# Weight slots and feature arrays at other byte phases in SBUF

## The chip, the cores and the metric

The kernel runs on one core of one Trainium2 chip, as one launch. The metric is device microseconds for the whole launch, the median of repeated executions. TensorE (PE) multiplies, VectorE (DVE), ScalarE (ACT) and GpSimd (POOL) do the elementwise work, SyncE (SP) and ScalarE issue DMAs. SBUF has 128 partitions; an address in this text is the byte offset within a partition, and "phase" is that address modulo 128 (or modulo 512, where said).

## What is computed

Two networks of layers on 512 tokens of 1024 features, all in float32. The first has four layers, each a mixer, a feed-forward block and a gated embedding; the second is one layer with a retention, a linear recurrence and a feed-forward block. Cut to what fills the time:

```python
for i in range(DEPTH):                       # DEPTH = 4
    y = mixer_i(h)                           # diff_attention, hgrn2, swa_sink_attention, diff_attention
    h = layer_norm(ALPHA * h + y, ln_g[i, 0], ln_b[i, 0])
    u = jnp.square(jax.nn.relu(h @ w_up[i])) @ w_down[i]      # 1024 -> 4096 -> 1024
    h = layer_norm(ALPHA * h + u, ln_g[i, 1], ln_b[i, 1])
    h = h + jax.nn.sigmoid(h @ w_ple_gate[i]) * (p[i] @ w_ple[i])
...
z = rms_norm_2(x, norm1_w) @ w_in            # second network: eight projections,
                                             # retention, RG-LRU, merge, feed-forward of 3072
```

Every large product is a projection: features (512 tokens) times a weight matrix that is read once from HBM.

## The kernel before

**Slabs.** All weights come as a stream of 287 slabs (`stream`, `N_SLABS`). A slab is 128 partitions x 8 x 256 floats (1 MB): 8 chunks k of 128 input features, for 256 output features. `Plan` lists them in the order of use; a unit is the work on one slab that ends in two PSUM banks.

**Slots.** A slab lives in one of four slots (`SLOT`, `make_slots`). A slot has two arrays of 8 KB a partition: `raw` (the slab as it lands), over which `wlo` is written in place, and `whi`. `place_slot` lays them out, one after the other; slots 0, 1 and 2 stand first in SBUF, slot 3 behind the constants. For slabs 211 to 249 slot 3 is used for other data and three slots turn.

**Split precision.** A float32 product is made of three float32r products. For the weights, SP's DMA fills `raw` (L433, after `unit_done` shows that the slot's previous slab is no longer needed); POOL rounds it into `whi` (L467; for 13 slabs ACT does it, L1340); DVE subtracts, `wlo = raw - whi` (L1767), and signals `split_done`, on which PE waits at the start of a unit (`begin_unit`). The features have two parts as well: `xh` and `xl`, `gh` and `gl`, 8 chunks of 512 floats each.

**Matmul shapes.** `feature_chunk` (L497 to L499 through `passes`): weights stationary (128x128), features moving, 512 columns; 48 matmuls a slab. `half_chunk` (L618 to L620): the same with 256 tokens at a time, used around the norms; 48 a slab for each half. `token_chunk` (L530 to L532): features stationary, 256 columns of weights moving; 96 a slab. In program order one matmul follows the other, high x high, high x low, low x high, and the weight load of each runs beside the matmul before it. Of 512 columns there are 8,976 matmuls from slots 0 to 2 and 2,160 from slot 3 (L497 to L499); of 256 columns 3,264 from slots 0 to 2 (2,304 in half chunks, 960 in token chunks) and 1,536 from slot 3 (960 and 576).

**Where a unit stands.** In a feed-forward block the slabs turn through the slots in order. In layer 0's block slab 18 (slot 2), 19 (slot 3), 20 (slot 0), 21 (slot 1), 22 (slot 2) and 23 (slot 3) are used in whole units one after the other, from 291.56 us of the profile on.

**Addresses.** `place` puts arrays one after the other from byte 16512, rounded up to 32 bytes. So raw0, whi0, raw1, whi1, raw2, whi2, h, xh, xl, gh and gl all lie at 128 modulo 512 (phase 0 modulo 128). The array `vec` has a size that is no multiple of 128; what stands behind it (ident, ones, small, raw3 at 151232, whi3 at 159424 and the arena of the mixers) lies at 192 modulo 512, phase 64 modulo 128. Each chunk of weights is 1024 bytes behind the one before, each chunk of features 2048, and the second half of a slab's outputs 512, so chunks have the phase of their array. No phase enters the order of work: it is written out by hand, with semaphores between the engines, and stays as it is.

Of the kernel before, what the change touches and what calls it, by code (L numbers as in the profile page):

```python
# [18 lines left out]
F32 = mybir.dt.float32  # L19
F32R = mybir.dt.float32r  # L20
# [4 lines left out]
P = 128  # L25
# [14 lines left out]
LAM_INIT = [0.8 - 0.6 * math.exp(-0.3 * i) for i in (0, 3)]  # L40
RD = 639
RING = 4

# [69 lines left out]
def make_slots():  # L115

    slots, users = [], {i: -1 for i in range(RING)}
    three = range(PLAN.at["ret"][0] + 2, PLAN.at["wout"][0] + 3)
# [8 lines left out]
SLOT = [s for s, _ in SLOTS]  # L127
# [17 lines left out]
def cols(hf):  # L145
    return slice(0, S) if hf is None else slice(hf * HALF, (hf + 1) * HALF)
# [64 lines left out]

def build(nc, stream, xin, pin, pos, vecs, relb, onehot, eye, picks, decay, out):
    with ExitStack() as ctx:
        top = [16512]

        def place(name, shape, dt=F32, at=None):

            size = (int(np.prod(shape[1:])) * 4 + 31) // 32 * 32
            if at is None:
                at, top[0] = top[0], top[0] + size  # L220
            assert at + size <= nc.sbuf_usable_end, (name, at, size)
            return nc.alloc_sbuf_tensor_at(name, shape, dt, offset=at)

        raw, wlo, whi = [], [], []

        def place_slot(i):
            at = top[0]
            raw.append(place(f"raw{i}", [P, 8, 256]))
            wlo.append(place(f"wlo{i}", [P, 8, 256], F32R, at=at))
            whi.append(place(f"whi{i}", [P, 8, 256], F32R))  # L230

        for i in range(3):
            place_slot(i)
        h = place("h", [P, KT, S])
        hg_m = place("hg_m", [P, 2, S], at=top[0] + 6 * S * 4)
        xh = place("xh", [P, KT, S], F32R)
# [5 lines left out]
        ident = place("ident", [P, P])  # L242
        ones = place("ones", [P, P])
        small = place("small", [P, 256])
        fourth = top[0]
        place_slot(3)
        arena = top[0]

# [10 lines left out]
        a = Arena()  # L259
# [7 lines left out]
        a = Arena(ln_end)  # L267
# [3 lines left out]
        a = Arena(ln_end)  # L271
# [5 lines left out]
        pair_end = a.at - arena  # L277
        sg = Arena(sg_at)("sg", [P, 2, 2, S])

        a = Arena()  # L280
# [12 lines left out]
        a = Arena()  # L293
# [13 lines left out]
        a = Arena()  # L307
# [9 lines left out]
        a = Arena(fourth - arena)  # L317
# [10 lines left out]
        rt_z = a("rt_z", [P, 2, S])  # L328
        rt_t = Arena(rt_z_at)("rt_t", [P, 2, S])
        rt_o = a("rt_o", [P, 4, 256])  # L330
        assert a.at - arena >= pair_end
        cosf = a("cosf", [P, S])
        sinf = a("sinf", [P, S])

# [2 lines left out]
        a = Arena(fourth - arena)  # L337
# [7 lines left out]
        a = Arena(ln_end)  # L345
# [4 lines left out]
        a = Arena(40 * 1024)  # L350
# [3 lines left out]
        a = Arena(sq_at)  # L354
# [14 lines left out]
        def sem(name):  # L369
            return ctx.enter_context(nc.semaphore(name))  # L370

        raw_in = [sem(f"raw_in{i}") for i in range(RING)]
        hi_done, hi_act = sem("hi_done"), sem("hi_act")
# [15 lines left out]
        def M(name):  # L389
            if name not in m:  # L390
                m[name] = sem(name)
            return m[name]
# [23 lines left out]
        @block.sync  # L416
        def _(sp):

            for t in range(4):
                sp.dma_start(raw[0][:, 2 * t:2 * t + 2].rearrange("p k n -> p (k n)"), stream[0, :, 512 * t:512 * t + 512]).then_inc(first_in[t], 16)  # L420
            for n in range(1, N_SLABS):
                if n < 3:
                    sp.wait_ge(x_in[n + 1], 16)
                elif n == 3:
                    sp.wait_ge(raw_in[2], 16)
                else:
                    sp.wait_ge(unit_done, PLAN.last_unit[BEFORE[n]] + 1)
                if n == RETURNED:
                    sp.wait_ge(gl_ready, 4 * (G_GEN["mixed"] + 1))
                if n == 2:  # L430
                    for dst, src in (vec[:, :], vecs), (ident[:, :], eye), (tab[:, :], onehot), (rb[0:32, :], relb):
                        sp.dma_start(dst, src).then_inc(loaded, 16)
                sp.dma_start(raw[SLOT[n]][:, :, :].rearrange("p k n -> p (k n)"), stream[n]).then_inc(raw_in[SLOT[n]], 16)  # L433

            for hf in range(2):
                for t in range(KT // 2):
                    p2 = slice(2 * t, 2 * t + 2)
                    sp.wait_ge(M("final_out"), KT // 2 * hf + t + 1)
                    sp.dma_start(out[:, p2, cols(hf)], fin[:, p2, cols(hf)]).then_inc(M("stored"), 16)
            sp.wait_ge(M("stored"), KT * 16)  # L440
# [2251 lines left out]
```

## Time and profile before

| | |
|---|---|
| median of 3 runs | 3551.46 us (3550.85 to 3552.41) |
| span of the profiled execution | 3552.2 us |
| PE busy | 3512.9 us (99%) |
| PE weight loads busy | 2952.0 us (83%) |
| DVE busy | 1766.9 us (50%) |
| ACT busy | 960.4 us (27%) |
| POOL busy | 632.3 us (18%) |
| granted TensorE clock | 0.998 of full |
| PE's share of the chain that ended last | 88% |

Busy time of PE is the union of its matmuls from issue to end. A matmul overlaps the next one, so its own duration (391 ns in the mean for 512 columns) is more than what it adds to the time. What it adds is the distance between starts, or a stretch of the profile divided by its matmuls.

### The profile page before, as it was taken

Reading aid. Unit: us, or ns where it says so; the run is one execution under the profiler, and the core shown is the slowest. Engines: PE = TensorE matmul, PEld = TensorE weight load, DVE = VectorE, ACT = ScalarE, POOL = GpSimd, SP = SyncE. Lnnn points to the kernel's source line nnn. Section 1 sums busy time; section 2 is a strip of 40 time slices with the busy share of each in tenths; the row PEclk is TensorE's granted clock in tenths of the full one; section 3 lists DMA queues with packets and bytes.
Section 4 is the critical chain, followed back from the end, with each engine's and each line's share of the span. In section 5 each row is a group of like instructions: output and inputs, shape, how many; then the busy total and the mean of one; then the engine's idle time right before and its main releaser. Section 6 shows DMA issues by size and latency. Waiting matters only on the chain.

```text
span 3552.2 us, 44299 instructions
## 1 busy us (share of the span) xinstructions
PE 3512.9 (99%) x18416; PEld 2952.0 (83%) x18416; DVE 1766.9 (50%) x2276; ACT 960.4 (27%) x1679; POOL 632.3 (18%) x372
## 2 busy tenths in 40 slices
PE   9999999999999999999999999999999999999999
PEld 7788888889888888688888878888888888898887
DVE  5454334556653346763336445553474346563434
ACT  3562001334220013630013256210141215120102
POOL 2112111200131112031112111311121111211110
PEclk9999999999999999999999999999999999999999
DMA  5322222222222223122222221222222222322222
GB/s 205 107 78 90 95 95 92 104 85 85 70 100 95 95 83 111 59 89 95 95 95 95 101 84 72 98 95 95 83 77 102 72 95 95 107 95 95 95 95 71
DMA packets 65463, 332.88 MB, mean 94 GB/s; under 512 B 9795, under 2 KB 20291, under 8 KB 28532
## 3 DMA queue, kind: packets, MB, share of 16 engines
q1 hardware_dynamic: 44316, 303.50, 23.8%
q10 hardware_dynamic: 20952, 26.56, 2.3%
q8 instruction: 149, 2.44, 0.3%
q14 instruction: 46, 0.38, 0.0%
HBM read 326.22 MB, written 10.90 MB: 95 GB/s over the span
## 4 chain that ended last, share of the span: by engine, by line
PE 88%; DVE 6%; ACT 4%; issue 1%; POOL 1%; DMA 0%; DVEq 0%; ACTq 0%; POOLq 0%
PE proj L497 23%; PE proj L499 23%; PE proj L498 23%; PE proj L618 2%; PE proj L619 2%; PE proj L620 2%; PE proj L530 2%; PE proj L532 2%; PE proj L531 2%; DVE wlo L1767 1%; PE mix L708 1%; DVE s L1877 1%; ACT xh L1182 1%; ACT h L1185 1%; PE mix L734 1%
## 5 line engine op out<-in xcount | busy, mean ns | idle before, releaser
L467 POOL TENSOR_SCALAR whi<-raw 128x2048 fp32r<-128x2048 f32 x272 | 528.8, 1944 | 2689.9 <-DVE wlo L1767 1722.1
L497 PE MATMUL proj<-gh,whi 128*128 128x512 f32 x1952 | 777.6, 398 | 2.2 <-DVE wlo L1767 2.2
L499 PE MATMUL proj<-gh,wlo 128*128 128x512 f32 x1952 | 763.5, 391 | 0.0
L498 PE MATMUL proj<-gl,whi 128*128 128x512 f32 x1952 | 762.8, 391 | 0.0
L1767 DVE TENSOR_TENSOR wlo<-raw,whi 128x2048 fp32r<-128x2048 f32 x285 | 651.3, 2285 | 137.9 <-POOL whi L467 95.2
L497 PE MATMUL proj<-xh,whi 128*128 128x512 f32 x1760 | 695.4, 395 | 8.9 <-DVE wlo L1767 3.1
L498 PE MATMUL proj<-xl,whi 128*128 128x512 f32 x1760 | 688.5, 391 | 0.0
L499 PE MATMUL proj<-xh,wlo 128*128 128x512 f32 x1760 | 688.4, 391 | 0.0
L497 PEld LDWEIGHTS proj<-gh,whi 128*128 128x128 f32 x1952 | 367.0, 188 | 95.1 <-issue 15.6
L499 PEld LDWEIGHTS proj<-gh,wlo 128*128 128x128 f32 x1952 | 366.9, 188 | 80.0
L498 PEld LDWEIGHTS proj<-gl,whi 128*128 128x128 f32 x1952 | 367.1, 188 | 77.7 <-issue 1.9
L497 PEld LDWEIGHTS proj<-xh,whi 128*128 128x128 f32 x1760 | 330.8, 188 | 92.5 <-issue 11.6
L499 PEld LDWEIGHTS proj<-xh,wlo 128*128 128x128 f32 x1760 | 330.9, 188 | 72.1
L498 PEld LDWEIGHTS proj<-xl,whi 128*128 128x128 f32 x1760 | 331.1, 188 | 70.9 <-issue 1.4
L1486 ACT ACTIVATE rl<-proj 128x1024 f32<-128x1024 f32 x64 | 65.8, 1028 | 957.1 <-PE proj L499 938.5
L1860 DVE TENSOR_TENSOR h<-h,proj 128x1024 f32<-128x1024 f32 (+1 forms) x76 | 80.0, 1053 | 351.8 <-PE proj L499 329.3
L2301 DVE SCALAR_TENSOR_TENSOR hid<-proj,rl 128x1024 f32<-128x1024 f32 x64 | 78.4, 1225 | 322.7 <-ACT rl L1486 322.2
L618 PE MATMUL proj<-xh,whi 128*128 128x256 f32 x608 | 174.3, 287 | 4.2 <-POOL xl L462 2.8
L619 PE MATMUL proj<-xl,whi 128*128 128x256 f32 x608 | 171.3, 282 | 0.0
L620 PE MATMUL proj<-xh,wlo 128*128 128x256 f32 x608 | 171.2, 282 | 0.0
L530 PE MATMUL proj<-whi,gh 128*128 128x256 f32 x512 | 149.0, 291 | 0.0
L532 PE MATMUL proj<-whi,gl 128*128 128x256 f32 x512 | 144.1, 282 | 0.0
(321 smaller groups left out, 4324.0 us busy)
## 6 DMA issues: line engine op xcount, KB each, us to landing
raw<-in_stream SPq DMA_DIRECT2D x286, 1024.0 KB, 4.8
da_b<-bias_da ACTq DMA_DIRECT2D x16, 512.0 KB, 3.4
bias_da<-bias_rows ACTq DMA_DIRECT2D x8, 512.0 KB, 8.8
h<-in_x ACTq DMA_DIRECT2D x4, 512.0 KB, 8.9
bias_sw<-bias_table ACTq DMA_DIRECT2D x1, 2048.0 KB, 9.9
pf<-in_p ACTq DMA_DIRECT2D x4, 512.0 KB, 6.8
sw_b<-bias_sw ACTq DMA_DIRECT2D x4, 512.0 KB, 3.6
out_features<-fin SPq DMA_DIRECT2D x8, 256.0 KB, 2.5
```

What stands on the lines that cost most here:

```text
L467: nc.gpsimd.tensor_scalar(whi[SLOT[n]][:, :, :], raw[SLOT[n]][:, :, :], 1.0, 0.0, ALU.mult, ALU.add).then_inc(hi_done, 1)
L497: nc.tensor.matmul(out, wh, ah, start=first, stop=False, skip_group_check=check)
L498: nc.tensor.matmul(out, wh, al, start=False, stop=False, skip_group_check=check)
L499: return nc.tensor.matmul(out, wl, ah, start=False, stop=last, skip_group_check=check)
L530: nc.tensor.matmul(o, ah, wh, start=k == 0 and st % per == 0, stop=False, skip_group_check=True)
L532: last = nc.tensor.matmul(o, al, wh, start=False, stop=k == kn - 1, skip_group_check=True)
L618: nc.tensor.matmul(o, wh, ah, start=k == 0 and (j if own_banks else hf) == 0, stop=False, skip_group_check=True)
L619: nc.tensor.matmul(o, wh, al, start=False, stop=False, skip_group_check=True)
L620: last = nc.tensor.matmul(o, wl, ah, start=False, stop=k == 7, skip_group_check=True)
L1767: V.tensor_tensor(wlo[SLOT[n]][:, :, :], raw[SLOT[n]][:, :, :], whi[SLOT[n]][:, :, :].bitcast(F32), ALU.subtract).then_inc(*own.sig(split_ ...
L1860: ins = V.tensor_tensor(o, o, y, ALU.add)
L2301: V.scalar_tensor_tensor(hid[:, :, :], banks(u), 0.0, rl[:, :, :], ALU.max, ALU.mult).then_inc(*own.sig(rel["dve"]))
```

## The change

The arrays of the slots get other addresses, in SBUF alone: what is loaded, computed and stored, and the order on every engine, are the same.

```diff
+STARTS = ((32, 64), (0, 0), (0, 0), (0, 256))
+ROWS = (256, 260, 258, 256)
...
-        top = [16512]
+        top = [16896]
...
         def place_slot(i):
-            at = top[0]
-            raw.append(place(f"raw{i}", [P, 8, 256]))
-            wlo.append(place(f"wlo{i}", [P, 8, 256], F32R, at=at))
-            whi.append(place(f"whi{i}", [P, 8, 256], F32R))
+            (lo, hi), row = STARTS[i], ROWS[i]
+            size = 8 * 4 * row
+            wide = [f(name, [P, 8, row], dt, at=top[0] + at) for f, name, dt, at in
+                    ((place, f"raw{i}", F32, lo), (place, f"wlo{i}", F32R, lo), (place, f"whi{i}", F32R, lo + size + hi))]
+            for slots, tile in zip((raw, wlo, whi), wide):
+                slots.append(tile[:, :, 0:256])
+            top[0] += (2 * size + lo + hi + 127) // 128 * 128
 
         for i in range(3):
             place_slot(i)
+        top[0] = (top[0] + 511) // 512 * 512
         h = place("h", [P, KT, S])
...
         small = place("small", [P, 256])
+        top[0] = (top[0] + 511) // 512 * 512
         fourth = top[0]
         place_slot(3)
...
-        assert a.at - arena >= pair_end
+        a.at = max(a.at, arena + pair_end)
...
-                sp.dma_start(raw[SLOT[n]][:, :, :].rearrange("p k n -> p (k n)"), stream[n]).then_inc(raw_in[SLOT[n]], 16)
+                sp.dma_start(raw[SLOT[n]][:, :, :], stream[n].rearrange("p (k n) -> p k n", k=8)).then_inc(raw_in[SLOT[n]], 16)
```

What comes out, modulo 128, for chunk k of a slab:

| | raw, wlo before | whi before | raw, wlo after | whi after |
|---|---|---|---|---|
| slot 0 | 0 | 0 | 32 | 96 |
| slot 1 | 0 | 0 | 16k | 16k |
| slot 2 | 0 | 0 | 8k | 64 + 8k |
| slot 3 | 64 | 64 | 0 | 0 (256 modulo 512) |

Modulo 512, h, xh, xl, gh and gl go from 128 to 0; ident, ones and small from 192 to 64; the arena of the mixers from 192 to 256. In slots 1 and 2 a partition of a slab is no longer one run of 8192 bytes but eight of 1024 with 16 or 8 bytes between them, so its DMA has 1,024 pieces in place of 128, and POOL's, ACT's and DVE's operands are 8 x 256 in place of 2048 elements. Slots 0 and 3 stay contiguous.

## Rows read from the trace of the kernel before

**Rows 1.** The page: busy time by engine; the chain that ended last.

```profile
PE 3512.9 (99%) x18416; PEld 2952.0 (83%) x18416; DVE 1766.9 (50%) x2276; ACT 960.4 (27%) x1679; POOL 632.3 (18%) x372
...
PE 88%; DVE 6%; ACT 4%; issue 1%; POOL 1%; DMA 0%; DVEq 0%; ACTq 0%; POOLq 0%
```

**Rows 2.** Groups of PE's matmuls: count, busy us, mean ns, idle before and who ended it.

```profile
L497 PE MATMUL proj<-gh,whi 128*128 128x512 f32 x1952 | 777.6, 398 | 2.2 <-DVE wlo L1767 2.2
...
L497 PE MATMUL proj<-xh,whi 128*128 128x512 f32 x1760 | 695.4, 395 | 8.9 <-DVE wlo L1767 3.1 <-DVE xl L2167 2.5 <-POOL xl L462 1.6
```

**Rows 3.** Stretches of one slab, 48 matmuls of 512 columns: slots 3, 0, 1, 3.

```profile
core 0: us, PE busy (x) PEld busy (x) DVE busy (x) ACT busy (x) POOL busy (x), PEclk, DMA share, GB/s
...
302.47:313.67 11.20, 11.20 (x49) 9.02 (x48) 5.79 (x4) 2.09 (x2) 2.83 (x1) 1.00 0.26 96
313.67:324.58 10.91, 10.91 (x50) 9.01 (x48) 4.65 (x3) 2.09 (x2) 1.92 (x1) 1.00 0.27 96
324.58:335.46 10.88, 10.88 (x50) 9.01 (x48) 3.42 (x2) 0.00 (x0) 1.92 (x1) 1.00 0.28 96
...
346.34:357.54 11.20, 11.20 (x50) 9.02 (x48) 3.42 (x2) 0.00 (x0) 1.91 (x1) 1.00 0.24 94
```

**Rows 4.** Timeline in slot 3, then slot 1 (start us, us); then groups of the two slabs.

```profile
307.84 0.39 PE L499 MATMUL proj<-xh,wlo 128*128 128x512 f32 x1
308.07 0.40 PE L497 MATMUL proj<-xh,whi 128*128 128x512 f32 x1
308.31 0.39 PE L498 MATMUL proj<-xl,whi 128*128 128x512 f32 x1
...
329.79 0.39 PE L499 MATMUL proj<-gh,wlo 128*128 128x512 f32 x1
330.02 0.39 PE L497 MATMUL proj<-gh,whi 128*128 128x512 f32 x1
...
L497 PE MATMUL proj<-xh,whi 128*128 128x512 f32 x16 | 6.3, 396 | 0.0
...
L497 PE MATMUL proj<-gh,whi 128*128 128x512 f32 x16 | 6.2, 389 | 0.0
```

**Rows 5.** Stretches with 256 columns: slots 2, 3, 3 (48 matmuls); 0, 3 (96).

```profile
598.66:604.41 5.75, 5.75 (x50) 5.75 (x48) 5.41 (x4) 1.15 (x2) 0.00 (x0) 1.00 0.49 182
618.02:623.48 5.46, 5.46 (x51) 5.46 (x49) 4.84 (x9) 3.91 (x8) 1.48 (x2) 1.00 0.55 195
604.41:610.06 5.65, 5.65 (x50) 5.65 (x49) 5.41 (x5) 0.64 (x1) 1.92 (x1) 1.00 0.01 3
2668.91:2680.43 11.52, 11.52 (x99) 11.52 (x97) 8.79 (x6) 1.03 (x1) 3.80 (x2) 1.00 0.29 95
704.67:715.98 11.31, 11.31 (x97) 11.30 (x96) 0.00 (x0) 1.09 (x2) 0.00 (x0) 1.00 0.26 94
```

**Rows 6.** Timeline of PE where the weights of the next slab are late.

```profile
2990.72 0.39 PE L499 MATMUL proj<-xh,wlo 128*128 128x512 f32 x1
2992.66 0.50 PE L497 MATMUL proj<-gh,whi 128*128 128x512 f32 x1 [1.55 <-DVE wlo L1767]
```

**Rows 7.** DMA issues: count, KB each, median us to landing; then POOL's group.

```profile
raw<-in_stream SPq DMA_DIRECT2D x286, 1024.0 KB, 4.8
da_b<-bias_da ACTq DMA_DIRECT2D x16, 512.0 KB, 3.4
...
sw_b<-bias_sw ACTq DMA_DIRECT2D x4, 512.0 KB, 3.6
...
L467 POOL TENSOR_SCALAR whi<-raw 128x2048 fp32r<-128x2048 f32 x272 | 528.8, 1944 | 2689.9 <-DVE wlo L1767 1722.1 <-DMA raw<-in_stream 922.8 <-DVE s L1877 44.9
```

**Rows 8.** DVE: the split of a slab (min/median/max ns), and two shapes of 512.

```profile
L1767 DVE TENSOR_TENSOR wlo<-raw,whi x285: 2260/2285/2318, 23.9 to 3508.4; 128x2048 fp32r<-128x2048 f32 x143
...
L1921 DVE TENSOR_TENSOR h<-h,mix 128x512 f32<-128x512 f32 x48 | 33.0, 688 | 3.7 <-DVE h L1923 0.5
...
L2125 DVE TENSOR_TENSOR hg_q<-hg_q,hg_t 128x512 f32<-128x512 f32 x24 | 16.5, 688 | 13.0 <-PE mix L815 13.0
```

## The prediction, made before the result was known

> **What bounds the kernel now.** I read the page first: PE is busy for 3512.9 of 3552.2 us and holds 88% of the chain of work that ended last, while DVE (50%), ACT (27%), POOL (18%) and the DMA engines have room [rows 1]. The reader should see that a faster DVE, POOL or DMA gives nothing here, and that a change which moves nothing but addresses can only tell in the spacing of PE's matmuls. So I took the spacing apart next. Two shapes fill PE: 11,136 matmuls of 512 columns (six groups of 1952 or 1760, of which two stand in [rows 2]) and 4,800 of 256 columns. The means there are from issue to end of one matmul, which overlaps the next; the spacing has to be read from the starts, or from how long a slab of 48 matmuls lasts.
>
> The table of stretches gives that for single slabs in one steady feed-forward run, at full granted clock [rows 3]. A slab of 48 matmuls of 512 columns takes 10.88 us from slot 1 (226.7 ns each), 11.20 us from slot 3 (233.3 ns each), and 10.91 us from slot 0 right after slot 3. Nothing waits in any of them, and PE does the same work. DVE, ACT and POOL are busy to different degrees in these stretches, but slabs from slot 3 later in the same run cost 11.20 again with ACT idle (346.34 to 357.54), so their company is not the cause. The timeline shows it matmul by matmul: starts 0.23 us apart for slot 1, 0.23 or 0.24 for slot 3, and the means from issue to end, 389 ns against 396, say the same [rows 4].
>
> What sets slot 3 apart is its address. By the placement code raw0 to whi2 and xh, xl, gh, gl all lie at 128 modulo 512; raw3 and whi3 lie at 192 modulo 512, so 64 bytes off the features that stream through. In the 256-column shapes the sign turns [rows 5]: a slab of 48 takes 5.75 us (119.8 ns each) from slot 2, but 5.65 or 5.46 from slot 3; a slab of 96 token matmuls takes 11.52 from slot 0 and 11.31 from slot 3. So the phase of weights against features is worth 3% of a matmul, either way by shape. That is the only lever the change has.
>
> **How fast a 512-column matmul can be.** The matmul of L499 at 2990.72 us (slot 2) has no weight load beside it, because the next slab is late and the next matmul starts 1.94 us on [rows 6]: it still takes 0.39 us, like those of slot 1 in rows 4. So 226.7 ns looks like the pace of the moving stream alone, not a loss to weight loads that a better phase could give back. I take it as the floor for this shape. For 256 columns the floor shown is 5.46 us for a slab (113.7 ns).
>
> The Trainium skill (SBUF — State Buffer, "Who interferes with whom"; TensorE: Matmul & The Clock Gate, "Step-by-step: what each phase is for") says that the moving operand and LDWEIGHTS have independent read ports and that PE never waits on anyone. By that rule no placement could change PE's spacing, and the whole change would be worth its DMAs only; the 11.20 beside 10.88 in rows 3 speaks against it.
>
> **The change part by part.**
> - *Slot 3 to 0 and 256, features to multiples of 512.* The phase against the features becomes 0 modulo 128, like slots 0 to 2 before. 2,160 matmuls of 512 columns use slot 3: 45 slabs x (11.20 - 10.88) = 14.4 us gained. That 256 modulo 512 acts like 0 is an assumption; the trace holds no such pair, so the bounds are 14.4 and 0. The 256-column slabs of slot 3 lose what they had: 20 slabs of 48 x 0.10 to 0.29, I take 0.2, so 3.9 us; 6 token slabs x 0.21 = 1.3 us. Together 5.2 lost.
> - *Slots 0 to 2 off phase, 512 columns.* This is the large term: 8,976 matmuls, 187 slabs, now at the floor of 10.88. Slot 0: whi at 96, wlo at 32. Slot 1: rows of 1040 bytes, so chunk k starts at 16k modulo 128. Slot 2: rows of 1032 bytes, 8k for wlo and 64 + 8k for whi. The trace shows only 0 and 64. Bounds per slab: 0 (all of these act like 0) and 0.32 (all act like 64). Two readings put it between. If what counts is which half of 128 bytes a weight row starts in, slot 0 has two of three matmuls in the far half, slot 1 half of them, slot 2 two of three: about 0.6 x 0.32 = 0.19. And the slab after slot 3 pays 0.03 us to settle after one change of phase [rows 3]; slots 1 and 2 now change phase at each of 8 chunks, 8 x 0.03 = 0.24. I take 0.20: 187 x 0.20 = 37.4 us lost. Ends: 0 and 59.8.
> - *Slots 0 to 2, 256 columns.* 48 slabs of 48 and 10 of 96, now at the slow end. With the same share of 0.6 towards slot 3's times: 48 x 0.6 x 0.2 + 10 x 0.6 x 0.21 = 7.1 us gained. Ends: 0, and 48 x 0.29 + 10 x 0.21 = 16.0.
> - *DMAs of slots 1 and 2.* The row in SBUF is no longer contiguous, so a slab that came in 128 pieces of 8 KB comes in 1,024 of 1 KB. The nearest rows: 512 KB in 1 KB pieces (sw_b) lands in 3.6 us, in 2 KB pieces (da_b) in 3.4; a slab in 8 KB pieces in 4.8 [rows 7]. That puts a slab at some 5.2 to 7.2 us. The cover is PE itself: a slab is asked for when its slot is let go, two or three slabs of 10.88 us ahead, and PE waited for wlo 2.2 + 3.1 us in all [rows 2]. The slabs that are already late (one stands in rows 6) can lose half a microsecond each: 1 us lost, ends 0 and 6. If the cover were gone, each of 150 slabs would pay 0.4 to 2.4.
> - *DVE, POOL and ACT on rows of 260 and 258.* The split of a slab takes 2260 to 2318 ns on DVE over all slots, so slot 3's phase does nothing there, and an operation over two runs of 256 elements (L1921, 688 ns) costs what a run of 512 does (L2125, 688 ns) [rows 8]. Taken at 0; POOL is idle most of the time and waits 1722 us for DVE [rows 7], so even 10% on its 1944 ns would be hidden. The arena moves from 64 to 0 modulo 128 while ident, ones and small stay at 64: some hundreds of small matmuls, each a few ns either way, taken at 0 with 1 us on both sides.
>
> Sum: -14.4 + 5.2 + 37.4 - 7.1 + 1.0 = +22.1 us. The profiled execution (3552.2 us) is 0.7 above the median of 3551.46, so the shift goes on the median: 3551.5 + 22.1 = **3573.6 us**.
>
> **The rivals.**
> 1. *Every phase settles at the floor, and the time falls.* If what costs is exactly an offset of 64, and the others let the stream settle as at 0, slots 0 to 2 lose nothing at 512 columns and slot 3 gains. Then -14.4 + 5.2 + 1.0, and the 256-column slabs give 0 to 16: 3527 to 3543. For it: slot 3 shows that phases exist which are faster at 256 columns, and only one phase is shown slow at 512. Against: a slab needs 0.03 us to settle after one change, and slots 1 and 2 change at each chunk. It decides when the off-phase slabs cost less than about 0.08 us over 10.88, since 187 x 0.08 = 15 is what the other terms give back. The Trainium skill (SBUF — State Buffer, "Specifications (TRN2)") gives SBUF lines of 16 bytes, with a penalty for each crossing to a new one; by that, slots 0 and 1, whose rows start at multiples of 16, would cost nothing, and no row here shows a line of that size.
> 2. *Worse than slot 3.* A single matmul in slot 3 takes 0.23 or 0.24 by turns; its mean of 233.3 ns is then made of turns of about 231 and 236. If an odd phase holds the slow turn, a slab takes 11.33: 187 x 0.45 = 84, and the time is about 3605 to 3635.
> 3. *No change.* Only if the slot 3 effect comes from something other than the phase, or the terms cancel (share of 0.2 in place of 0.6): 3551.5 + 1 = 3552, within 7 us. The Trainium skill's rule of independent ports, named above, gives the same time.
> 4. *The DMAs bind.* 1 KB pieces slow a slab beyond the cover: PE's waits for wlo would grow from 5.3 us to tens, in the stretch with three slots (2700 to 3110 us) first. 3575 to 3600; small, since even with three slots the cover is 2 x 10.88 - 4.8 - 1.9 - 2.3 = 12.8 us (slab, load, POOL and DVE from rows 3, 7 and 8).
>
> **How the numbers follow.** The forecast case (a loss of 0.1 to 0.32 us a slab in slots 0 to 2: 3558 to 3600) gets 0.47. Rival 1 gets 0.25, rival 2 0.10, rival 3 0.14, rival 4 0.04. A range that holds 8 in 10 starts inside rival 1, at 3530, and ends at the bound of the forecast case with a slot 3 that gains little, 3605. The likeliest case alone: 3558 to 3600. A measurement here tells about 0.2% (7 us) from no change: faster than 3544.4 in 0.25, within in 0.15 (rival 3 and an edge of the forecast case), slower than 3558.6 in 0.60.
>
> **What would show it.** In the changed profile, 48-matmul slabs in the same feed-forward run: slot 3 at 10.88 (right) or still 11.20 (256 does not act like 0); slots 0, 1, 2 at 11.0 to 11.2, and within slots 1 and 2 a spacing that differs from chunk to chunk. 256-column slabs from slots 0 to 2 between 5.46 and 5.75. DVE's split still 2285 ns, slab DMAs 5 to 7 us, PE's waits for wlo below 10 us. The prediction is wrong if slots 0 to 2 stay at 10.88, or if they go below it: then 226.7 ns was no floor, and the gain would be of a size that nothing above allows for.

## The result, and the profile of the changed kernel

The changed kernel takes 3589.02 us (3587.55 to 3589.61, 4 runs) beside 3551.81 us (3550.85 to 3552.41, 4 runs) of the kernel before on the same chip: ratio 1.0103, 95% interval 1.0089 to 1.0116, so 37.2 us slower. The profiled execution has a span of 3587.6 us, where before had 3552.2. Direction and mechanism were as predicted, and the time is inside the range. The shift was put at 22.1 us, so its largest term had been put too small.

The page of the changed kernel, to be read beside [rows 1], [rows 2] and [rows 7]: busy time by engine; the queue of the slabs (packets, MB, share of 16 engines); the chain that ended last; a group of matmuls; the slabs' DMA. L497 to L499 of before are L504 to L506 here.

```profile
PE 3549.2 (99%) x18416; PEld 2952.2 (82%) x18416; DVE 1764.6 (49%) x2276; ACT 960.3 (27%) x1679; POOL 631.9 (18%) x372
...
q1 hardware_dynamic: 178716, 303.50, 25.4%
...
PE 87%; DVE 6%; ACT 4%; issue 1%; POOL 1%; DMA 0%; DVEq 0%; ACTq 0%; POOLq 0%
...
L504 PE MATMUL proj<-gh,whi 128*128 128x512 f32 x1952 | 785.1, 402 | 1.8 <-DVE wlo L1774 1.8
...
raw<-in_stream SPq DMA_DIRECT2D x286, 1024.0 KB, 5.5
```

PE is 36.3 us longer busy (3512.9 before) with the same 18,416 matmuls; DVE, ACT and POOL do what they did. A matmul of the group takes 402 ns from issue to end where it took 398. The table below shows that the shift of 35.4 us in the span is PE's spacing.

Stretches of one slab in the same feed-forward block of layer 0 (columns as in [rows 3]): slots 3, 0, 1, 2 at 512 columns; then 48 matmuls of 256 columns from slots 2 and 3, and 96 token matmuls from slot 3.

```profile
303.15:314.04 10.89, 10.89 (x50) 9.01 (x48) 5.79 (x4) 2.09 (x2) 2.82 (x1) 1.00 0.32 99
314.04:325.31 11.27, 11.27 (x49) 9.02 (x48) 4.65 (x3) 2.09 (x2) 1.92 (x1) 1.00 0.26 93
325.31:336.48 11.17, 11.17 (x49) 9.03 (x48) 3.42 (x2) 0.00 (x0) 1.90 (x1) 1.00 0.26 94
336.48:347.64 11.16, 11.16 (x50) 9.02 (x48) 3.42 (x2) 0.00 (x0) 1.90 (x1) 1.00 0.32 95
...
603.40:609.08 5.68, 5.68 (x49) 5.67 (x48) 5.34 (x4) 1.15 (x2) 0.00 (x0) 1.00 0.60 185
609.08:614.84 5.76, 5.76 (x51) 5.76 (x50) 5.52 (x5) 0.63 (x1) 1.91 (x1) 1.00 0.01 3
710.19:721.70 11.51, 11.51 (x98) 11.51 (x97) 0.00 (x0) 1.09 (x2) 0.00 (x0) 1.00 0.30 93
```

The roles have changed: slot 3, 11.20 before [rows 3], is now at 10.89, and slots 0, 1 and 2, 10.88 to 10.91 before, are at 11.27, 11.17 and 11.16. At 256 columns slot 3 is now the slow one (5.76, and 11.51 for a token slab, 11.31 before [rows 5]) and slot 2 gains a little (5.68, 5.75 before).

What PE waited for (us in total, times, longest), and DVE's split of a slab (min/median/max ns):

```profile
PE proj L504 <- DVE wlo L1774: 3.9, 7, 1.4
```

```profile
L1774 DVE TENSOR_TENSOR wlo<-raw,whi x285: 2260/2284/2319, 25.1 to 3543.7; 128x2048 fp32r<-128x2048 f32 x143
```

PE's waits for `wlo` are not longer than before (3.9 us in all, where [rows 2] had 2.2 and 3.1), and the split takes what it took [rows 8].

Where the time went, by laying the matmuls of both profiles side by side in program order and adding up the differences between starts (only where neither has a gap behind it):

| | matmuls | mean spacing before, after (ns) | us |
|---|---|---|---|
| slot 0, 512 columns | 2,922 | 227.6, 234.4 | +19.8 |
| slot 1, 512 columns | 2,955 | 227.1, 232.7 | +16.4 |
| slot 2, 512 columns | 2,923 | 227.3, 232.3 | +14.8 |
| slot 3, 512 columns | 2,163 | 233.2, 227.1 | -13.2 |
| slot 3, 256 columns | 1,481 | | +4.7 |
| slots 0 to 2, 256 columns | 3,120 | | -4.8 |
| all the rest, gaps included | | | -2.0 |
| sum | | | +35.7 |

The sum runs from the start of the first matmul to the start of the last. Within slot 1 the mean spacing of a chunk lies between 230.1 and 235.3 ns, within slot 2 between 229.6 and 234.7. Chunk 0 of slot 1, whose `whi` lies at the features' phase and whose `wlo` lies 128 bytes off, has 232.8 ns.

### The profile page after: what moved, and what is told of

The parts are those of the page before. It is cut to its first block, busy times and chain, and to the rows that moved or that the text cites. A ratio compares the mean times of both kernels' runs of the same rounds, so it can differ in the third digit from the quotient of the medians.

```text
span 3587.6 us, 44299 instructions
## 1 busy us (share of the span) xinstructions
PE 3549.2 (99%) x18416; PEld 2952.2 (82%) x18416; DVE 1764.6 (49%) x2276; ACT 960.3 (27%) x1679; POOL 631.9 (18%) x372
## 4 chain that ended last, share of the span: by engine, by line
PE 87%; DVE 6%; ACT 4%; issue 1%; POOL 1%; DMA 0%; DVEq 0%; ACTq 0%; POOLq 0%
PE proj L504 23%; PE proj L506 23%; PE proj L505 23%; PE proj L625 2%; PE proj L626 2%; PE proj L627 2%; PE proj L537 2%; PE proj L538 2%; PE proj L539 2%; DVE wlo L1774 1%; PE mix L715 1%; DVE s L1884 1%; ACT xh L1189 1%; ACT h L1192 1%; PE mix L741 1%
## 5 line engine op out<-in xcount | busy, mean ns | idle before, releaser
L504 PE MATMUL proj<-gh,whi 128*128 128x512 f32 x1952 | 785.1, 402 | 1.8 <-DVE wlo L1774 1.8
L506 PE MATMUL proj<-gh,wlo 128*128 128x512 f32 x1952 | 770.3, 395 | 0.0
L505 PE MATMUL proj<-gl,whi 128*128 128x512 f32 x1952 | 769.7, 394 | 0.0
L504 PE MATMUL proj<-xh,whi 128*128 128x512 f32 x1760 | 700.3, 398 | 7.2 <-DVE xl L2174 2.5
L506 PE MATMUL proj<-xh,wlo 128*128 128x512 f32 x1760 | 693.3, 394 | 0.0
L505 PE MATMUL proj<-xl,whi 128*128 128x512 f32 x1760 | 692.8, 394 | 0.0
L504 PEld LDWEIGHTS proj<-gh,whi 128*128 128x128 f32 x1952 | 367.3, 188 | 100.8 <-issue 15.6
L506 PEld LDWEIGHTS proj<-gh,wlo 128*128 128x128 f32 x1952 | 367.7, 188 | 87.2
L505 PEld LDWEIGHTS proj<-gl,whi 128*128 128x128 f32 x1952 | 367.1, 188 | 84.3 <-issue 1.9
L504 PEld LDWEIGHTS proj<-xh,whi 128*128 128x128 f32 x1760 | 330.7, 188 | 95.4 <-issue 11.1
L506 PEld LDWEIGHTS proj<-xh,wlo 128*128 128x128 f32 x1760 | 331.0, 188 | 77.7
L505 PEld LDWEIGHTS proj<-xl,whi 128*128 128x128 f32 x1760 | 330.5, 188 | 75.9 <-issue 1.4
L538 PE MATMUL proj<-wlo,gh 128*128 128x256 f32 x512 | 144.3, 282 | 0.0
```

Of the source, the lines that this page charges most:

```text
L504: nc.tensor.matmul(out, wh, ah, start=first, stop=False, skip_group_check=check)
L505: nc.tensor.matmul(out, wh, al, start=False, stop=False, skip_group_check=check)
L506: return nc.tensor.matmul(out, wl, ah, start=False, stop=last, skip_group_check=check)
L538: nc.tensor.matmul(o, ah, wl, start=False, stop=False, skip_group_check=True)
```

## The experiments

Theory at the start: the spacing of PE's matmuls follows from the distance in bytes between the array of the weights and that of the features, and the slabs' DMAs and the other engines add nothing. Rival theories: the absolute address counts; the change of phase from chunk to chunk costs; the shorter DMA pieces cost. Each kernel is the kernel before with the edit shown. "At d" means that a weight array lies d bytes off the features.

**Slot 3 alone, at the features' phase.**

```diff
+        def align(phase):
+            top[0] += (128 + phase - top[0]) % 512
...
+        align(0)
         fourth = top[0]
         place_slot(3)
```

> The kernel before with slot 3 moved to 128 modulo 512, the phase of the features and of the other slots; everything else stays (the arena moves with it). If the relation of weights to features is what counts, slot 3's slabs of 48 matmuls of 512 columns go from 11.20 to 10.88 us (45 slabs, 14 us) and its 256-column slabs from 5.46 or 5.65 to 5.75 and from 11.31 to 11.52 (5 us lost): 3542 to 3544 us. If slot 3 was slow for another reason (its place behind the constants, its neighbours in the arena), it stays at 11.20 and the time at 3551.

Measured: 3540.06 beside 3552.74 us, ratio 0.9965 (0.9952 to 0.9977): 12.7 us faster. Slots 2 and 3 in the feed-forward block:

```profile
335.04:345.92 10.88, 10.88 (x50) 9.01 (x48) 3.42 (x2) 0.00 (x0) 1.91 (x1) 1.00 0.28 98
345.92:356.80 10.88, 10.88 (x50) 9.01 (x48) 3.42 (x2) 0.00 (x0) 1.92 (x1) 1.00 0.25 96
```

Slot 3's 512-column matmuls give 13.5 us, its 256-column ones take 4.7, and some 4 us of the two spans' difference come from elsewhere (1.4 us from the spacing in slots 0 to 2, whose slab behind slot 3 took 10.91, the rest from gaps). The first term of the prediction stands, and it is the part of the change that was worth having.

**The 1 KB pieces alone.** The stream is stored with rows of 260 elements for slots 1 and 2, so that their slabs go in 1,024 pieces to the old, contiguous places.

```diff
+                if SLOT[n] in (1, 2):
+                    of = of.rearrange("p (k n) -> p k n", k=8)[:, :, 0:256]
```

> The kernel before with only the DMAs of slots 1 and 2 in 1 KB pieces: in HBM the chunks of a row stand 1040 bytes apart, in SBUF nothing moves. If the DMAs carry a part of the loss of 37 us, the time is above 3555. If they are covered by PE, as the theory of phases says, landing goes from 4.8 to some 6 us and the time stays within 2 us of 3552.

Measured: 3552.82 beside 3552.74 us, ratio 1.0002 (0.9993 to 1.0011). Its queue and the DMA of a slab:

```profile
q1 hardware_dynamic: 178716, 303.50, 26.0%
...
raw<-in_stream SPq DMA_DIRECT2D x286, 1024.0 KB, 5.4
```

As many packets as in the changed kernel, a landing 0.6 us later than before [rows 7], and no time beyond the interval of -2.5 to +3.9 us: the DMAs are out as the cause of 37 us.

**One phase for all chunks of a slot, by turns.** Both kernels keep rows of 256 elements and shift whole slots: slots 0 to 3 at 16, 32, 48, 0 in one, at 80, 96, 112, 8 in the other.

```diff
+PHASE = (16, 32, 48, 0)
...
+            align(PHASE[i] // 32 * 32)
```

> Slots 0, 1 and 2 at 16, 32 and 48 bytes past the phase of the features, rows of 256, so that phase is the same in every chunk and for whi and wlo; slot 3 at the features' phase. A theory that the changes of phase from matmul to matmul cost (0.03 us each) gives 10.88 to 10.91 us a slab in all four slots, and some 3540 us. A theory that the phase itself costs gives 11.0 to 11.3 us for slots 0 to 2 and 10.88 for slot 3, near 3575.

> The same with slots 0 to 3 at 80, 96, 112 and 8 bytes past the features. If changes of phase cost, all four at 10.88 to 10.91 us and some 3540 us. If the phase itself costs, 11.0 to 11.3 us a slab, slot 3 with its 8 bytes too, near 3585. If only the 64-byte half counts, 8 is like 0 (10.88) and the others like 64 (11.20).

Measured in one execution each: 3575.49 and 3596.18 us, beside 3552.74. Stretches of slots 0, 1, 2 of the first, then 0 to 3 of the second, in the feed-forward block:

```profile
314.05:324.94 10.89, 10.89 (x49) 9.01 (x48) 4.65 (x3) 2.09 (x2) 1.91 (x1) 1.00 0.27 96
324.94:336.13 11.19, 11.19 (x49) 9.01 (x48) 3.42 (x2) 0.00 (x0) 1.92 (x1) 1.00 0.26 94
336.13:347.33 11.20, 11.20 (x49) 9.12 (x48) 3.42 (x2) 0.00 (x0) 1.91 (x1) 1.00 0.26 95
```

```profile
314.50:325.64 11.14, 11.14 (x49) 9.01 (x48) 4.65 (x3) 2.09 (x2) 1.93 (x1) 1.00 0.23 94
325.64:336.89 11.25, 11.25 (x50) 9.04 (x48) 3.42 (x2) 0.00 (x0) 1.92 (x1) 1.00 0.26 93
336.89:348.09 11.20, 11.20 (x50) 8.98 (x49) 3.42 (x2) 0.00 (x0) 1.90 (x1) 1.00 0.26 95
348.09:359.16 11.07, 11.07 (x50) 9.02 (x49) 3.42 (x2) 0.00 (x0) 1.92 (x1) 1.00 0.26 95
```

A slot at 32 or 48 costs 11.19 and 11.20 with the same phase in all its chunks, as much as slots 1 and 2 of the changed kernel (11.17, 11.16), whose phase changes at each chunk. So no change of phase from chunk to chunk is needed for this price. Nor does it turn on the half of 128 bytes in which a row begins: 32 costs what 64 did.

**Everything at one other phase.** All slots, the features and the arena are moved by 64 bytes together.

```diff
+PHASE = (64, 64, 64, 64)
...
+        align(64)
```

> All four slots and the features 64 bytes on, at 192 modulo 512, rows of 256. If the relation of weights to features counts, all slots take 227 ns a matmul at 512 columns and the time is 3540 us. If the address itself counts (a weight row that starts in the second half of 128 bytes), all slots take 233 ns: 11,136 x 6.3 = 70 us more, near 3605.

Measured: 3541.62 us in one execution, within 2 us of the kernel with slot 3 aligned, at another absolute address. Slot 0 and slot 3:

```profile
311.62:322.50 10.88, 10.88 (x49) 9.01 (x48) 4.65 (x3) 2.09 (x2) 1.91 (x1) 1.00 0.26 96
...
344.26:355.14 10.88, 10.88 (x49) 9.01 (x48) 3.42 (x2) 0.00 (x0) 1.91 (x1) 1.00 0.27 96
```

So the absolute address is out: what counts is how far the weights lie from the features.

**The parts of the change, each alone.** Both kernels are the changed one with one table set back: slot 0's part without the rows, and the rows without slot 0's part.

```diff
-ROWS = (256, 260, 258, 256)
+ROWS = (256, 256, 256, 256)
```

> The changed kernel with rows of 256 in every slot: slot 0 keeps 32 and 96, slots 1 to 3 are at the features' phase. From the spacing in the changed kernel, slot 0's 2928 matmuls of 512 columns cost 7.3 ns each more (21 us) and its 256-column ones give 2 us back, so if the parts add up this is 3540 + 19 = 3559 to 3561 us. If the losses of the changed kernel come from jumps between slots of different phase instead, slot 0 alone costs less than 10 us.

```diff
-STARTS = ((32, 64), (0, 0), (0, 0), (0, 256))
+STARTS = ((0, 0), (0, 0), (0, 0), (0, 256))
```

> The changed kernel with slot 0 at 0 and 0: rows of 260 and 258 in slots 1 and 2 stay. If the parts add up: 3024 x 5.7 + 3024 x 5.1 = 33 us on 3540, less 3 us from 256 columns: 3569 to 3571 us, and with slot 0's part the 37 us of the change are whole. If rows that change phase at each chunk disturb slot 0 and 3 too, more, and slot 0's 512-column matmuls are above 228 ns.

Measured: 3589.32 us (ratio 1.0102, 1.0087 to 1.0118) and 3572.13 us (ratio 1.0054, 1.0039 to 1.0069), beside 3553.21. The second is 1 us above what was expected; the first is 28 us above it, as slow as the whole change. Its slots 0 and 1:

```profile
314.35:325.62 11.27, 11.27 (x49) 9.02 (x48) 4.65 (x3) 2.09 (x2) 1.92 (x1) 1.00 0.26 93
325.62:336.78 11.16, 11.16 (x50) 9.04 (x48) 3.42 (x2) 0.00 (x0) 1.90 (x1) 1.00 0.26 94
```

Slot 1 is contiguous here, at a multiple of 128 from the features, and was to take 10.88; it takes 11.16. With slot 0 using 128 bytes more, slots 1 and 2 lay at 33408 and 49792, which is 128 modulo 256, and the features at 0. The assumption of a period of 128 bytes had fallen, and a period of 256 took its place as the theory.

**A period of 256 bytes?** Slots 0 to 3 at 128, 256, 192 and 0:

```diff
+PHASE = (128, 256, 192, 0)
```

> The kernel before with slot 0 at 128, slot 1 at 256, slot 2 at 192 bytes off the features (modulo 512) and slot 3 at 0, rows of 256 elements, offsets the same in all chunks; nothing left out. If the distance counts modulo 128 (the prediction's reading): slots 0, 1 and 3 space their 512-column matmuls 226.7 to 227.2 ns, slot 2 some 233 (the 64 of slot 3 before), in all 2992 x 6 ns = 18 us on the 3540 of the run with slot 3 aligned, 3558. If it counts modulo 256 (what the run of slot 0's part alone points to): slot 0 is off as well, 232 to 234 ns, slot 1 is not, time 3571 to 3577. If it counts modulo 512: slot 1 is off too, 3585 to 3595.

Slots 0 to 3:

```profile
311.73:322.89 11.16, 11.16 (x50) 9.04 (x48) 4.65 (x3) 2.08 (x2) 1.91 (x1) 1.00 0.26 95
322.89:333.77 10.88, 10.88 (x49) 9.01 (x48) 3.42 (x2) 0.00 (x0) 1.91 (x1) 1.00 0.25 96
333.77:344.76 10.99, 10.99 (x50) 9.02 (x48) 3.42 (x2) 0.00 (x0) 1.90 (x1) 1.00 0.26 97
344.76:355.64 10.88, 10.88 (x49) 9.01 (x48) 3.42 (x2) 0.00 (x0) 1.91 (x1) 1.00 0.26 96
```

128 is slow and 256 is not. A period of 128 bytes is out, and one of 256 fits (the next kernels bear it out). The time, 3555.98 us in one execution, was below the 3571 to 3577 expected, because 192 costs only a third of what 64 does: 10.99 here beside 11.20 [rows 3]. The two are not the same distance, as they would be modulo 128, nor is the effect symmetric.

And slot 0's part again, now with slots 1 and 2 at multiples of 256:

```diff
+STARTS = ((32, 64), (128, 0), (0, 0), (0, 256))
+ROWS = (256, 256, 256, 256)
```

> Slot 0's 32 and 96 and the features at multiples of 512 as in the change, with slots 1, 2 and 3 at 0 modulo 256 off the features (the earlier run of slot 0's part had slots 1 and 2 at 128). If the distance counts modulo 256: slots 1 to 3 space 226.7 to 227.2 ns at 512 columns and slot 0 234.4, so 2928 x 7.2 ns = 21 us on 3540, less 1 to 2 us at 256 columns: 3557 to 3561, ratio 1.0015 to 1.003. If the neighbours in the run before were slow for another reason (the place of slot 0, the features at 0 modulo 512), it stays at 3585 to 3590.

Measured: 3561.59 beside 3553.52 us, ratio 1.0023 (1.0013 to 1.0032): the ratio is as expected, the time 0.6 us above the range. Slots 0 and 2:

```profile
312.40:323.68 11.28, 11.28 (x50) 9.02 (x48) 4.65 (x3) 2.08 (x2) 1.92 (x1) 1.00 0.27 93
...
334.58:345.46 10.88, 10.88 (x49) 9.01 (x48) 3.42 (x2) 0.00 (x0) 1.92 (x1) 1.00 0.27 98
```

The parts now add up within the noise: slot 3 at the features' phase -12.7 us; slot 0, 8.1 + 12.7 = +20.8; the rows of 260 and 258 (which start at 0 off the features there, and 128 off in the changed kernel), 18.9 + 12.7 = +31.6. Together +39.7, beside 37.2 measured, with 3 to 5 us of uncertainty on each ratio.

**Each slab at the distance that its shape wants.** Rows 3 and 5 showed that 64 slows 512 columns and speeds 256. Every slab is used in one shape, so a slab can lie where its shape is fast, by an offset inside a slot that is a little larger.

```diff
+            top[0] += (top[0] % 128 and 128 - top[0] % 128)
...
+            o = PHASE[n] // 4
+            for views, tile in zip((raw, wlo, whi), wide[SLOT[n]]):
+                views.append(tile[:, o:o + 2048].rearrange("p (k n) -> p k n", k=8))
```

> A faster version, if the map of phases holds: each slot has 128 bytes to spare for raw and whi, and a slab is put by how it is used: 0 bytes past the features for 512 columns, 64 for the 34 slabs of half chunks, 112 for the 16 token slabs. From the spacings read so far: 34 x 96 x (119.8 - 116.0) = 12 us and 16 x 96 x (119.8 - 114.1) = 9 us below 3540, so 3517 to 3523. If the 256-column spacings depend on what slabs come before, less of it; under 3540 in any case.

Measured: 3590.07 beside 3553.21 us, ratio 1.0105 (1.0088 to 1.0122), a miss by 67 us. Slot 0 at 512 columns, then 48 matmuls of a half slab:

```profile
312.36:323.57 11.21, 11.21 (x50) 9.02 (x48) 4.65 (x3) 2.09 (x2) 1.90 (x1) 1.00 0.26 94
```

```profile
603.00:608.44 5.44, 5.44 (x49) 5.43 (x48) 5.10 (x4) 1.15 (x2) 0.00 (x0) 1.00 0.57 193
```

The slots were aligned modulo 128 only, so that in slots 0 to 2 `raw` and `wlo` lay at 0 and `whi` at 128 modulo 256 off the features: slow at 512 columns. Modulo 512 these slots differ (256 and 384 in slots 0 and 2, 0 and 128 in slot 1), and their slabs of 48 do not: 11.21 and 11.19 beside 11.20. That is more evidence for the period of 256. By the same slip half slabs had one array at 64 and one at 192, and took 5.44, against 5.65 and 5.46 with both at 64 [rows 5] and 5.65 with both at 192 (slot 2 of the kernel with the offsets 128, 256 and 192).

Slot 3 lay the other way round, with `whi` at 0 and `wlo` at 128, and that separates the three matmuls of a chunk. The groups of one slab there (columns as in [rows 2]; L511 to L513 are L497 to L499 of before), and a matmul with the weight load that runs beside it:

```profile
L513 PE MATMUL proj<-gh,wlo 128*128 128x512 f32 x17 | 6.8, 397 | 0.0
L512 PE MATMUL proj<-gl,whi 128*128 128x512 f32 x16 | 6.3, 396 | 0.0
L511 PE MATMUL proj<-gh,whi 128*128 128x512 f32 x16 | 6.2, 389 | 0.0
```

```profile
350.35 0.40 PE L512 MATMUL proj<-gl,whi 128*128 128x512 f32 x1
350.35 0.19 PEld L513 LDWEIGHTS proj<-gh,wlo 128*128 128x128 f32 x1
```

The second group in the kernel with slot 3 aligned, where it is L505:

```profile
L505 PE MATMUL proj<-gl,whi 128*128 128x512 f32 x16 | 6.2, 389 | 0.0
```

The matmul of `whi` and `gl` has its own operands at distance 0 in both kernels. Beside it the weights of the next matmul are loaded, out of `wlo`. With `wlo` at 0 it takes 389 ns and the next one starts 227.0 ns on; with `wlo` at 128 it takes 396, and 232.4 ns pass. So this price comes with the array whose weights are loaded beside the features that stream, and not with the matmul's own weights. That is not the whole rule. The matmul of `wlo` itself, beside which `whi` at 0 is loaded, is slow too (397, and 234.8 ns to the next start). Nor do the two arrays add up: a third of the matmuls at 128 would make 10.97 us of a slab and two thirds 11.07, by the 10.88 and 11.16 above, but the slabs take 11.10 and 11.21. A difference between the distances of `whi` and `wlo` has a price of its own.

The next kernel keeps 64 and 192 for half slabs and aligns the rest modulo 256.

```diff
+BY_SHAPE = {"whole": (0, 0), "half": (64, 192), "token": (112, 112)}
...
+            top[0] += (128 - top[0]) % 256
```

> All four slots and the mixers' arena at 0 modulo 256 off the features, and each slab laid in its slot at an offset that its matmul shape wants: whole slabs 0 and 0, half slabs wlo 64 and whi 192, token slabs 112 and 112; nothing left out. If the distance counts modulo 256: 512 columns at 226.7 to 227.2 ns, half chunks 114.2 in place of 119.8 (34 x 96 x 5.6 ns = 18 us), token chunks 114 to 117 in place of 119.8 (1536 x 3 to 6 = 4 to 9 us), so 3540 less 22 to 27: 3510 to 3520, ratio 0.988 to 0.991. If the loss at 512 columns in the first run of this kind had another cause (the offset inside a slot, changing per slab), it stays near 3590.

Measured: 3528.41 beside 3553.52 us, ratio 0.9929 (0.9915 to 0.9942). Slot 1 at 512 columns, 48 matmuls of a half slab, 96 of a token slab:

```profile
320.16:331.04 10.88, 10.88 (x50) 9.01 (x48) 3.42 (x2) 0.00 (x0) 1.91 (x1) 1.00 0.27 96
...
592.16:597.60 5.44, 5.44 (x49) 5.44 (x48) 5.11 (x4) 1.15 (x2) 0.00 (x0) 1.00 0.59 193
...
697.09:708.01 10.92, 10.92 (x98) 10.92 (x96) 0.00 (x0) 1.09 (x2) 0.00 (x0) 1.00 0.28 98
```

These slabs run at the best pace seen for their shapes, and yet the time is 8 us above the upper end of what was expected. Side by side with the kernel with slot 3 aligned (span 3539.1, here 3527.2), the spacing gives 14.6 us in half slabs and 7.8 in token slabs, 22.5 in all. 9.7 us of it are given back in the 60 us from the start of each run of half slabs on, where PE now comes early and waits; 0.9 us lie elsewhere. The same 401 matmuls around a norm of the second network, first with slot 3 aligned, then here; and what the two kernels wait for in them:

```profile
2605.93:2656.89 50.96, 48.60 (x402) 47.98 (x401) 39.00 (x58) 20.01 (x33) 5.58 (x3) 1.00 0.23 83
```

```profile
PE mix L601 <- DVE s L1884: 2.3, 2, 1.3
```

```profile
2596.35:2648.72 52.37, 48.50 (x402) 47.80 (x400) 38.94 (x58) 20.14 (x33) 5.58 (x3) 0.97 0.23 79
...
2612.00:2616.00 4.00, 2.38 (x15) 2.38 (x16) 1.72 (x4) 2.96 (x5) 0.00 (x0) 0.82 0.02 4
2616.00:2618.00 2.00, 2.00 (x11) 2.00 (x11) 0.00 (x0) 1.09 (x2) 0.00 (x0) 0.52 0.00 0
```

```profile
PE mix L612 <- DVE s L1895: 3.5, 2, 2.1
```

The faster matmuls made this stretch 1.4 us longer. PE reaches DVE's `s` sooner and waits 2.14 us, and behind that wait the granted clock is down (0.82 in the mean of the 4 us from 2612 on, 0.52 in the 2 us from 2616 on). The timeline of PE before and behind it, start and duration in us:

```profile
2611.20 0.28 PE L638 MATMUL proj<-xh,wlo 128*128 128x256 f32 x1
2613.62 1.27 PE L612 MATMUL mix<-ones,s 128*128 128x128 f32 x8 [2.14 <-DVE s L1895]
...
2615.34 0.41 PE L636 MATMUL proj<-xh,whi 128*128 128x256 f32 x1
2615.55 0.41 PE L637 MATMUL proj<-xl,whi 128*128 128x256 f32 x1
...
2618.73 0.28 PE L638 MATMUL proj<-xh,wlo 128*128 128x256 f32 x1
```

Starts are 0.21 us apart from 2614.9 on, where 0.11 is the pace, until the clock is back near 2618: the engine ran at 1.2 in place of 2.4 GHz for some 3.5 us.

**Is that the faster pace, or chance?** The eight half slabs at the two places that lost most (slabs 71 to 74 and 207 to 210) go back to the slow distance 0.

```diff
+EARLY = (71, 72, 73, 74, 207, 208, 209, 210)
```

> The kernel of phase_by_shape_2 with the eight half slabs 71 to 74 and 207 to 210 laid back to the offset 0; the other 26 half slabs and the token slabs keep theirs; nothing left out. These eight stand before and behind the two places where phase_by_shape_2 lost 2.2 and 2.4 us against slot3_aligned (at about 940 and 2612 us), where PE comes early, waits 1.7 and 2.1 us for DVE's s, and the granted clock reads 0.5 behind the wait. Theory (the wait and the clock behind it eat the gain there): the dip near 2612 us is gone and the wait for s near it is back at 1.3 us and below, the spacing of these slabs is 119.8 ns again (8 x 96 x 5.2 ns = 4 us lost), and 3 to 5 us of waits and slow matmuls come back, so the time is the same within 2 us: 3526 to 3530. Rival (waits and clock are chance, not made by the earlier arrival): the 4 us are lost and nothing comes back, 3532 to 3533.

Measured: 3527.07 beside 3552.43 us, ratio 0.9927 (0.9911 to 0.9944). The same 401 matmuls, the stretch in which the clock had been low, and the waits:

```profile
2596.99:2647.95 50.96, 48.60 (x402) 48.00 (x401) 39.00 (x58) 20.00 (x33) 5.59 (x3) 1.00 0.23 83
2612.00:2616.00 4.00, 2.71 (x24) 2.51 (x23) 2.32 (x5) 2.43 (x5) 0.00 (x0) 1.00 0.02 4
```

```profile
PE mix L613 <- DVE s L1896: 2.3, 2, 1.3
```

The clock stays at 1.00, the wait is 1.3 us again, and the stretch is 50.96, as with slot 3 aligned. The time lies where the theory put it (3526 to 3530), but its interval reaches the rival's ratio of 0.994 as well; it is the trace that speaks for the theory, with the wait back at its old length at the place that was changed. At the other place, near 940 us, the wait for `s` went from 1.7 to 0.3 us, and 0.6 us came back. The clock still fell there behind another wait of 2.5 us (for `xl`), and behind the same wait it had stayed at 1.00 in the kernel with slot 3 aligned. In the kernel before, with slow half slabs, it fell there as well behind a wait of 2.55 us for `xl` (0.50 from 948 to 950 us). So that the longer wait is made by the earlier arrival is shown, in one profiled execution of each kernel; how surely the clock follows is not.

## Why the prediction was right in sign and too small

*What bounds the kernel.* Right. The change moved addresses alone, and 35.4 us of span went to PE's spacing, with PE's busy time up by 36.3.

*Slot 3 to 0 and 256.* Right in both parts: -13.2 us at 512 columns for -14.4, and +4.7 at 256 for +5.2. The assumption that 256 acts like 0 holds (10.89, and 10.88 with all of slot 1 at 256).

*Slots 0 to 2, 512 columns: the term that failed.* It was put at 0.20 us a slab, 37.4 us, and measured 51.0 us, 0.27 a slab. For slots 0, 1 and 2 (61, 63 and 63 slabs) that is 12.2, 12.6 and 12.6 us predicted, and 19.8, 16.4 and 14.8 measured. Two steps behind it were false.

The first is the share of 0.6, taken from the reading that a row costs only when it starts in the far half of 128 bytes. A start at 32 costs as much as one at 64 (11.19 us a slab), so `wlo` of slot 0 was not free, and one at 96 costs more (11.25). With `wlo` at 32 and `whi` at 96 a slab takes 11.27, which is 0.36 above its 10.91, so slot 3's 0.32 was no upper bound either. This slot makes 7.6 of the 13.6 us that were missed, and none of its arrays lies at a multiple of 128.

The second is the phase of 0 modulo 128 counted as free: the distance counts modulo 256. In the changed kernel `raw1` and `wlo1` start at 128 modulo 256 off the features, and so does chunk 0 of `raw2`. Chunk 0 of slot 1, all at phase 0 modulo 128, has a spacing of 232.8 ns, where that reading has the 227.1 of before. How the other 6.0 us divide between the two steps is not worked out.

The other reading, 0.03 us for each change of phase between chunks, had come out near the same 0.2 by chance: 11.19 and 11.20 are paid without any such change. What holds is this: with both weight arrays at one distance, 0 is free and 16 nearly so (10.88 and 10.89 here, 227.1 and 228.5 ns in the mean over the whole kernel), 8 costs 0.19 us a slab, 192 costs 0.11, and the others tried, from 32 to 128, cost 0.26 to 0.37. Where the two arrays differ, the slab's time does not follow from these prices alone.

*Slots 0 to 2, 256 columns.* Predicted -7.1 us, measured -4.8. The share of 0.6 was too large here: half slabs in these slots have 117.8 to 118.2 ns, where 0 gives 119.8 and 64 gave 116.0, a share of some 0.45.

*DMAs.* Predicted +1.0 with bounds 0 and 6; the run with the pieces alone gives 0.1, with slabs landing at 5.4 us. The landing of 5.2 to 7.2 us was right, and so was the cover.

*DVE, POOL, ACT at nothing.* Right: the split is 2260/2284/2319 ns.

*The floor of 226.7 ns.* No kernel went below 10.88 us a slab at 512 columns. At 256 columns the floor is 113.3 ns (5.44 us), not 113.7.

*The rivals.* Rival 1 (every phase settles at the floor) is out for most distances; it nearly holds for 16. Its threshold of 0.08 us a slab was passed more than threefold. Rival 2 (11.33 a slab) is out: the slowest slab shown takes 11.28. Rival 3 is out. The Trainium skill (SBUF — State Buffer, "Who interferes with whom") says that the moving operand and the weight load have ports of their own and that PE waits on nobody, and by that no placement would matter. The traces do not agree: 10.88 beside 11.28 us for the same 48 matmuls, by distance alone. Rival 4 is out by the run with the pieces. The sum, term by term: 22.1, and 13.6 more for slots 0 to 2 at 512 columns, 2.3 for their smaller gain at 256, 1.2 and -0.5 for slot 3, and -3.0 for all the rest (-2.0 in place of +1.0), make the 35.7 us of the two profiled executions; the medians are 37.2 apart, within their interval.

The same page of the Trainium skill ("Specifications (TRN2)") has lines of 16 bytes with a penalty for crossing one. The pair of 8 (11.07) and 16 (10.89) would agree with it; 32 to 128, all multiples of 16 and all slow, are not explained by it.

What stays open is what collides. The runs show that the distance between weights and features counts modulo 256, and with the opposite sign for some distances at 256 columns. They show one matmul, with its own operands at distance 0, that slows when the weights loaded beside it come from an array at 128. They do not show why the matmul behind it is slow as well, why the two weight arrays act on each other, or what stands behind the period. Distances between 128 and 256 other than 192 were not tried with both arrays alike.

## What to carry to other kernels

Where PE is bound by back-to-back matmuls, give all weight arrays and the moving arrays the same phase modulo 256 bytes, whatever that phase is; here that was worth 0.35%, and a misplacement cost 1%. Look for a group of matmuls whose spacing differs from its twins in another buffer, and compare the buffers' addresses before anything else; test the period with a few uniform offsets before building on it. A gain in pace pays only where PE is not about to wait: around half slabs 9.7 of 22.5 us were given back, some of it through a clock that was low behind the longer wait.

## What was not expected of the hardware

- A distance of 128 bytes is slow (11.16 us a slab) and one of 256 is free (10.88), so a placement that looks aligned to 128 bytes is off by half a period.
- 192 is not the mirror of 64: 10.99 beside 11.20.
- At 256 columns the distances 64 and 192 for the two weight arrays run at 113.3 ns a matmul in the slab shown, where 0 runs at 119.8: 5.44 beside 5.75 us for 48. With both at 64, or both at 192, a slab shown took 5.65.
- A matmul whose own two operands lie at distance 0 takes 389 ns, and 396 when the weights loaded beside it come from an array at 128.
- Behind a wait of 2.14 us the granted clock of PE was at 0.52, behind one of 1.3 us at the same place at 1.00; a stretch whose half-slab matmuls had become some 5% faster took 1.4 us longer.
